# Attention in two forms: the product with the values split into two column halves, and another schedule for a search's counts

## The reference, cut to what matters

```
def forgetting_attention(q, k, v, log_f):            # "fox"
    for start in range(0, S, Q_BLOCK):               # Q_BLOCK = 128
        end = start + Q_BLOCK
        s = einsum('bqhd,bkhd->bhqk', q[:, start:end], k[:, :end]) * scale
        s = s + Ft[:, :, start:end, None] - Ft[:, :, None, :end]
        s = where(tk <= tq, s, -inf)
        p = softmax(s, axis=-1)
        outs.append(einsum('bhqk,bkhd->bqhd', p, v[:, :end]))

def dsa_attention(q, k, v, qi, ki, wi):              # one k and v head for all 8 heads
        score = einsum('bqh,bqhk->bqk', wi, relu(einsum('bqhd,bkd->bqhk', qi, ki)))
        _, idx = top_k(where(allowed, score, -inf), kk)      # kk = min(256, end)
        kg, vg = gather(k[:, :end], idx), gather(v[:, :end], idx)
        p = softmax(where(valid, einsum('bqhd,bqkd->bhqk', q, kg) * scale, -inf))
        outs.append(einsum('bhqk,bqkd->bqhd', p, vg))
```

## Time and profile before

| | us |
|---|---|
| median of 3 runs | 3101.83 |
| lowest, highest | 3099.99, 3105.59 |
| the profiled execution's own time | 3098.0 |
| its span | 3095.9 |
| busy PE, DVE, ACT, POOL in the span | 2754.6, 2152.0, 1280.4, 774.9 |
| mean granted clock of PE | 0.934 of full |

### The profile page before, as it was taken

The page is one execution under the profiler, slowest core; times in us unless marked ns, Lnnn a source line. Parts: engine busy times, 40 slices in busy tenths (PEclk is TensorE's granted clock), DMA queues, the critical chain, the costliest instruction groups (busy, mean ns, idle before and its releaser), DMA issues.

```text
span 3095.9 us, 35168 instructions
## 1 busy us (share of the span) xinstructions
PE 2754.6 (89%) x12924; PEld 2207.4 (71%) x12924; DVE 2152.0 (70%) x2892; ACT 1280.4 (41%) x2069; POOL 774.9 (25%) x385
## 2 busy tenths in 40 slices
PE   6999989979588869969979996989899489999998
PEld 3788767755365658858767875777788478888887
DVE  5589865526689944854634898973555479999997
ACT  3233321110166631223224214666532067777775
POOL 1432310000111100000210006555200035566664
PEclk9999999988798889989989998999999689999999
DMA  6222347633454452326543247441232289999996
GB/s 224 77 70 84 104 148 239 204 126 124 158 184 169 176 229 68 102 56 153 105 116 83 99 112 135 110 121 25 89 123 97 116 310 381 381 383 384 388 381 222
DMA packets 236294, 530.82 MB, mean 171 GB/s; under 512 B 30742, under 2 KB 147590, under 8 KB 219859
## 3 DMA queue, kind: packets, MB, share of 16 engines
q1 hardware_dynamic: 173058, 435.96, 40.2%
q0 software_dynamic: 33680, 58.97, 7.8%
q10 hardware_dynamic: 29376, 33.56, 3.1%
HBM read 450.74 MB, written 95.48 MB: 176 GB/s over the span
## 4 chain that ended last, share of the span: by engine, by line
PE 51%; DVE 6%; POOL 2%; ACT 2%; DMA 2%; issue 1%; SPq 1%; DVEq 0%; ACTq 0%; POOLq 0%
PE banks L143 47%; PE banks L153 4%; DVE a_P L2163 1%; DVE c_rows L1518 1%; POOL a_P L2187 1%; ACT a_PT L2206 1%; DVE m_w_low L1621 0%; DVE e_low L2666 0%; POOL a_R L1551 0%; DMA i_q<-iqT 0%; DVE a_R L1556 0%; ACT m_w_low L1614 0%; DMA p_low_raw<-in_w_out 0%; DMA odsaT<-a_o 0%; ACT e_high L2660 0%
## 5 line engine op out<-in xcount | busy, mean ns | idle before, releaser
L2666 DVE TENSOR_TENSOR e_low<-e_raw,e_high 128x4096 fp32r<-128x4096 f32 x99 | 437.9, 4425 | 64.1 <-ACT e_high L2660 64.1
L143 PE MATMUL banks<-m_w_low,p_high 128*128 128x512 f32 (+1 forms) x1248 | 381.0, 389 | 13.3 <-DVE m_w_low L1621 13.3
L2660 ACT ACTIVATE e_high<-e_raw 128x4096 fp32r<-128x4096 f32 x99 | 359.5, 3633 | 26.9 <-DVE e_g L2615 26.9
L143 PE MATMUL banks<-h_high,w 128*128 128x512 f32 (+1 forms) x1024 | 297.9, 373 | 9.1 <-POOL w L373 4.4
L505 DVE SCALAR_TENSOR_TENSOR acc<-img,taps,acc 128x1024 f32<-128x1024 f32 x160 | 259.8, 1625 | 61.6 <-ACT acc L483 56.6
L143 PEld LDWEIGHTS banks<-m_w_low,p_high 128*128 128x128 f32 x1248 | 234.3, 195 | 57.4 <-issue 8.7
L143 PE MATMUL banks<-m_w_low,p_low 128*128 128x512 f32 (+1 forms) x624 | 240.5, 385 | 0.0
L143 PEld LDWEIGHTS banks<-h_high,w 128*128 128x128 f32 x1024 | 186.2, 191 | 49.0 <-POOL w L373 4.9
L143 PE MATMUL banks<-e_high,e_xhigh 128*128 128x512 f32 x528 | 211.5, 401 | 7.1 <-issue 5.5
L143 PE MATMUL banks<-e_high,e_xlow 128*128 128x512 f32 x528 | 208.3, 395 | 0.0
L143 PE MATMUL banks<-e_low,e_xhigh 128*128 128x512 f32 x528 | 207.9, 394 | 0.0
(11 more groups left out here) (495 smaller groups left out, 6245.5 us busy)
## 6 DMA issues: line engine op xcount, KB each, us to landing
e_raw<-in_exp_w SPq DMA_DIRECT2D x99, 2048.0 KB, 13.0
s_sums<-cumT SPq DMA_DIRECT2D x32, 768.0 KB, 4.5
w_raw<-in_w_in SPq DMA_DIRECT2D x20, 1024.0 KB, 6.2
s_X<-xtok SPq DMA_DIRECT2D x19, 1024.0 KB, 7.3
p_raw<-in_w_in SPq DMA_DIRECT2D x18, 1024.0 KB, 7.3
w_raw<-in_ada_w SPq DMA_DIRECT2D x12, 1024.0 KB, 5.4
mod_w<-in_ada_w SPq DMA_DIRECT2D x12, 1024.0 KB, 6.9
w_raw<-in_w_ada SPq DMA_DIRECT2D x10, 1024.0 KB, 8.1
```

The costliest lines, as they stand in the source:

```text
L143: last = pe.matmul(out, a, b, start=start and n == 0, stop=stop and n == len(pairs) - 1)
L2660: act.activation(self.high[p % HIGHS][:], self.raw[p % RAWS][:], ACT.Copy).then_inc(*self.high_done.up())
L2666: dve.tensor_tensor(self.low[p % HIGHS][:], self.raw[p % RAWS][:], self.high[p % HIGHS][:].bitcast(F32), ALU.subtract).then_inc(*self.low_ ...
```

## The change

The product with the values is made for each head by itself. For each key block there are two f32 matmuls, each with that head's 64 value columns as weights and its 128 turned probabilities as moving columns; head 0's result goes to partitions 0 to 63 of the bank, head 1's to partitions 64 to 127, both in columns 0 to 127. The DSA values are kept and loaded once instead of twice, the output copy covers 128 columns instead of 256, and one DMA stores both heads. In the schedule of the search, fox pairs with five or more key blocks keep two items; all other pairs get one, those of the first two DSA query blocks too.

```diff
-        fv, dv = s.sb("a_fv", [P, NT, 512]), s.sb("a_dv", [P, NT, 2, HD])
+        fv, dv = s.sb("a_fv", [P, NT, 512]), s.sb("a_dv", [P, NT, HD])
...
-        o = [s.sb(f"a_o{b}", [P, 2, P]) for b in range(2)]
+        o = [s.sb(f"a_o{b}", [P, P]) for b in range(2)]
...
         def weigh_values(i):
             kind, j, c = pairs[i]
             z = i % 2
-            out = core.bank[:, 6 + z, 0:256]
             pe.wait_ge(*copy_done[i])
...
             if pairs[i] == ("dsa", 0, 0):
-                pe.wait_ge(*values_in[1].at(2))
+                pe.wait_ge(*values_in[1].at(1))
             if i >= 2:
                 pe.wait_ge(*out_free[i - 2])
-            products(pe, out, [(fv[:, k, P * c:P * c + P] if kind == "fox" else dv[:, k, :, :].rearrange("p a d -> p (a d)"),
-                                PT[z][:, k, :, :].rearrange("p e n -> p (e n)")) for k in range(j + 1)]).then_inc(*summed.up())
+            for k in range(j + 1):
+                for e in range(2):
+                    at = P * c + HD * e
+                    last = pe.matmul(core.bank[HD * e:HD * e + HD, 6 + z, 0:P], fv[:, k, at:at + HD] if kind == "fox" else dv[:, k, :], PT[z][:, k, e, :],
+                                     start=k == 0, stop=k == j)
+            last.then_inc(*summed.up())
             sum_done[i] = summed.now()
...
-                act.wait_ge(*stored[z].at(2 * (i // 2)))
-            act.activation(o[z][:].rearrange("p e n -> p (e n)"), core.bank[:, 6 + z, 0:256], ACT.Copy).then_inc(*closed.up())
+                act.wait_ge(*stored[z].at(i // 2))
+            act.activation(o[z][:], core.bank[:, 6 + z, 0:P], ACT.Copy).then_inc(*closed.up())
...
-            for e in range(2):
-                sp.dma_start(dram[f"o{kind}T"][P * c + HD * e:P * c + HD * e + HD, at], o[z][HD * e:HD * e + HD, e, :]).then_inc(*stored[z].up())
+            sp.dma_start(dram[f"o{kind}T"][P * c:P * c + P, at], o[z][:]).then_inc(*stored[z].up())
...
-        for half in range(2):
-            sp.dma_start(dv[:, :, half, :], pv[:, :, C_DV:C_DV + HD]).then_inc(*values_in[1].up())
+        sp.dma_start(dv[:], pv[:, :, C_DV:C_DV + HD]).then_inc(*values_in[1].up())
...
-            chosen.fill(2 if pairs[i][0] == "fox" else 0 if pairs[i][1] < TOPK // P else 1, R)
+            chosen.fill(2 if pairs[i][0] == "fox" and pairs[i][1] >= 4 else 1, R)
```

## The result

The changed kernel takes 3064.93 us (median of 4 runs, 3064.03 to 3068.1) against 3100.91 (3099.72 to 3105.59) for the kernel before: ratio 0.9883 (0.9866 to 0.99). Forecast were 3062 us and 3047 to 3099. The profiled execution of after took 3064.03 us, its span is 3062.1; that of before took 3098.0. The sum of the prediction was -39.5 us for the stage; from the first pair's reciprocal to the last attention store the stage became 38.55 us shorter (339.85 to 301.30). The rest of the span, whose code is the same, came out 4.7 us longer (3.04 ahead of the stage, 1.65 behind it).

A forecast was written before the change was run, and what follows sets the result against it. VectorE was taken to bound the fox passes and PE the heavier DSA passes; terms -19, -21.5, -1.5, +1 and +1.5 summed to -39.5 us, giving 3058.5 from the profiled execution, 3062 as median, range 3047 to 3099.

The forecast's parts named there:

- What bounds: Attention stage: VectorE bounds the fox passes, with PE close; PE bounds DSA passes of five or more key blocks.
- Values, concurrency: Value product: the two column halves stream at once, a key block taking 0.22 us instead of 0.432, 61 us of PE less.
- Rival 2: Value product: the halves take turns, 0.44 us a block, so almost nothing is gained; 3098 us (3094 to 3106), chance 0.20.
- Rival 3: Value product: a half's weights do not load while the other streams, 0.66 us a block; slower, 3154 us, chance 0.08.
- Fox, -19: Fox passes: 15 us less in 23 passes and 4 less in four earlier light ones, from the largest engine sums.
- The 4 us taken off as hidden twice: The 23 fox passes: the counted difference of 19 us was taken as 15, for what neighbouring passes already hide.
- DSA of five and more blocks, -21.5: DSA from 2101.19 us on: 223 value records save 24 us, 10% given back because ACT comes close; PE stays the bound.
- the first rival: Value product: halves stream at once, but each change of array mode costs a drain, 12 us in all; 3074 us, chance 0.20.
- Output copy: ACT's copy of the attention output, halved to 128 columns: 0.27 us instead of 0.380, 0.11 us less a pass.
- Three and four DSA blocks, -1.5: DSA passes of three and four blocks: 1.5 us less, since ACT and DVE are as late as PE there.
- Counts in light DSA passes, +1: DSA passes of one and two blocks: eight counts moved in are mostly covered, costing 1 us (bounds 0 and 4).
- The moved marks, +1.5: Two search marks move from passes of 4 and 5 blocks to 6 and 7: net +1.5 us (bounds -2 and +5).

The follow-up runs named there:

- e3: Changed kernel with the value matmuls issued head by head, all key blocks of head 0, then all of head 1: 3089.7 us, ratio 0.9982.
- e1: Changed kernel with the search's counts on the old schedule, so only the value product in two column halves is new: 3074.72 us, ratio 0.9937.
- e7: Changed kernel with each pair's value matmuls cut in two parts, ahead of and behind the turns, four mode changes a pass: 3066.88 us, one run.
- e5: Changed kernel with eight search counts left out, so the first eight DSA passes get none: 3063.57 us, ratio 0.9893.
- e2: Changed kernel with the old value product, output copy and stores, so only the schedule of counts is new: 3094.42 us, ratio 0.9988.
- e10: Changed kernel with value matmuls ordered two key blocks of one head, then two of the other: 3067.39 us, one run.
- e6: Changed kernel with each of the search's six marks split into three items and the schedule adjusted for twelve more items: 3072.25 us, ratio 0.9912.
- e4: Changed kernel with GpSimd's loads behind a head's last fox pair issued only after that pair's normalising: 3061.93 us, ratio 0.9888.
- e8: Changed kernel with GpSimd's loads spread, one or two issues a pass behind the normalising: 3058.6 us, ratio 0.987.

## Why the prediction was right

**What bounds.** Both bounds held as named. In fox the two runs with one part each show that PE and DVE were both at the edge. The largest of the engines' sums, added over eight passes, gave 39.7 us, measured are 38.7 (pairs 15 to 23); pass by pass it was not so good, as the fox term shows.

**Values, concurrency.** Right: 0.22 us a block, the end of the bounds that was chosen. The choice rested on an argument about columns and partitions, not on a row; e3 against after is what shows it. Rival 2's 0.44 us a block is measured in e3, with its order, and not in the changed kernel. Rival 3 (0.66) is refuted: 28 loads of half weights take 1.51 us under the 28 records, in the same rows of the array, so what the prediction quotes with that rival doesn't hold for these halves. Two sums there were off as well: rival 2's own terms (-4 and +2.5) give 3100 and not 3098, and rival 3 with 119 ns (four records of 0.228 us) about 3226 and not 3217.

**Fox, -19.** Measured -2.86 (pairs 3 to 8) and -16.35 (the 23 passes): -19.2. The four light passes of eight (new pair's j = 3 to 0) were forecast at 12.25 us (4.0, 3.3, 2.7, 2.25) and take 12.2 (3.21, 3.64, 3.12, 2.24), before 18.5. The pass of j = 4, which PE's sum put at 6.7 us before and 4.95 after, takes 4.54 both times: the heavy turns and values of PE show in the passes behind it (5.34 us at j = 2 before, forecast 4.6). For the 23 passes the text has a difference of 19 us; its own sums give 3 x (39.7 - 32.8) = 20.7. The light passes of these 23 gave 18.3 us, and 2.0 were lost again in two of the three passes with GpSimd's issues (3.3 in all three), which no step had. The 4 us taken off as hidden twice stood in for that loss and for a difference too large in the j = 4 passes: that the term fits to 0.2 us is luck. The lightest pass, timeline of DVE in after, to lay beside the last one of the earlier trace rows:

```profile
2013.69 0.17 DVE L2179 RECIPROCAL a_rc<-a_sm 128x2 f32<-128x2 f32 x1 [0.36 <-ACT a_P L2172]
...
2014.46 1.15 DVE L1518 TENSOR_SCALAR_CACHE_REDUCE c_rows<-c_rows,i_cand 128x896 bf16<-128x896 f32 x1
...
2015.93 0.17 DVE L2179 RECIPROCAL a_rc<-a_sm 128x2 f32<-128x2 f32 x1 [0.33 <-ACT a_P L2172]
```

One count, 2.24 us, and DVE waits 0.33 us for ACT at its end: 2.25 was forecast for it, with ACT as the bound.

**DSA of five and more blocks, -21.5.** From pair 46 to the last store e1, which has the old places of counts and marks, is 18.5 us shorter than before (105.95 against 124.47). Of the 24 us of PE's work 5.5 did not arrive, as much as 18 passes at the 0.3 us of e7. ACT, for which 2.4 us had been given back, is not what holds: PE is busy 27.84 of the last five passes' 29.10 us. So the first rival's mechanism was there beside the forecast's, at its price, and the text had treated the two as if one excluded the other. A pass of eight blocks is 5.99 us, forecast 5.7.

**Output copy.** 0.264 us by form in fox, forecast 0.27:

```profile
L2235 ACT ACTIVATE a_o<-banks 128x128 f32<-128x128 f32 x24 | 6.3, 264 | 0.0
```

**Three and four DSA blocks, -1.5.** Measured -0.73.

**One and two DSA blocks, the halves.** No term; measured -1.6 (e1, 20.61 against 22.19).

**Counts in light DSA passes, +1.** Mis-sized: +4.2 beside e1. "Where a pass is now as short as 1.7 the cover is gone" was the right mechanism, but the base was 2.8 us a pass, 22.19 divided by eight, and the stretch has nine passes: 2.5; with the halves it is 2.3 (20.61 us for nine), and the count's 1.15 to 1.28 us has no cover in most. It is 0.2 over the upper bound of 4; 1.7 of it stay in e5, where the counts are gone.

**The moved marks, +1.5.** Wrong in sign. The working's own terms give (9.9 - 4.4) + (11.5 - 5.1) - (9.2 - 3.1) - (10.8 - 4.9) = -0.1, and +1.5 was set above them without a row. The runs: pairs 46 to 63 shrink by 4.8 us from before to e2 and by 2.7 from e1 to after.

The chain of after through the first moved mark (start us, us, what), a pass of 11.26 us, forecast 9.9:

```profile
2094.20 2.53 POOL a_R L1551
...
2096.75 2.04 DVE a_R L1556
...
2098.81 1.16 DVE a_R L1557
...
2100.00 1.16 DVE c_rows L1558
...
2101.24 0.94 POOL c_rows L1560
```

The two passes of the marks last 11.26 and 11.64 us, before 9.18 and 10.78: 2.94 more, forecast 1.4. But the passes that they vacate last 3.28 and 3.26, not 3.1 and 4.9, since the turns and values in a pass of five blocks' scores are those of lighter pairs before it; and those that they displace would last 4.63 and 5.29 (e1). That is -3.38, together -0.4. The other 2.3 lie in passes around: the two behind the old place are 1.0 us shorter without the marks, the two behind the new one 1.0 shorter with them (9.39 against e1's 10.42), 0.3 in pairs 50 to 54. Why a mark shortens the passes behind it by more among heavy pairs was not tested.

**The sum.** In us: -19.2 fox; -1.6 and +4.2 in the lightest DSA passes; -0.7; -18.5; -2.7 for the marks: -38.5, forecast -39.5. Three terms were off by 3 to 4 us, two of them up (counts, mode changes) and one down (marks), and the fox term hid its errors in itself. The mechanism of the gain was right; that the time came out within 3 us of the forecast is in part luck.

## What to carry over

Two engines that both fill a stretch are relieved together or not at all: 6.65 and 3.31 us alone were 16.35 in the pair, so take a bound per pass for each engine and sum the largest over a whole cycle of passes; single passes can be off (6.7 us for 4.5 here). When passes shrink, read again what was hidden in them by its length, DMA issues in one piece on an engine that also computes, and the landing of stores when there are few output buffers. When a schedule is moved, look which instructions come to lie beside GpSimd's. Where a matmul uses half of the array's columns, put records of the two halves next to each other; the same records in two rows one behind the other gained nothing.

## What the runs showed of the hardware

- Records of 64 weight columns in the two column halves run beside each other: 0.22 us for two pairs of 128 moving columns (after, e10), 0.44 when all records of one half come first (e3).
- The order need not be strictly alternating: two by two is as good to 0.05 us a product (e10); at the border of two long rows about three records overlap (e3).
- A change between whole array and halves and back costs about 0.3 us (after, e7), some 0.09 ahead of the first half record and 0.2 behind the last one, where the first whole load is no longer hidden.
- A half's weight load is shown with 137 ns (before: 190 for the full one) and does not limit a pair of records every 0.109 us.
- A DMA issue holds GpSimd for 0.57 to 0.81 us here, six in a row for 3.8, and the compute instructions queued behind wait for all.
- The small int32 instruction of DVE that opens a round, median 0.17 us in after's fox passes, lasted until GpSimd had ended, to 0.04 us, wherever it started while GpSimd normalised: 15 of 31 in after's stage, up to 2.08 us, and 21 of 31 in e6's, up to 1.74.
- A store of 64 KB landed 1.6 us after its issue in the median and up to 7.4 us after it in the stretch of light DSA passes (after, 2000 to 2050 us); with two output buffers, landings of 6.0 to 6.4 us stand on the chains of after, e4 and e8.
